# Streaming most of a kernel's modulation weights beside its first mixer instead of ahead of it

## What is computed

```python
def modulation(cond, w_ada, b_ada):
    m = jax.nn.silu(cond) @ w_ada + b_ada
    return jnp.split(m[:, None, :], 6, axis=-1)

for l in range(DEPTH):
    sh1, sc1, g1, sh2, sc2, g2 = modulation(cond, P['w_ada'][l], P['b_ada'][l])
    h = rms_norm(x, P['norm_mix'][l]) * (1 + sc1) + sh1
    out, new = even_mixer(...)          # layer 1: odd_mixer
    x = x + g1 * out
    h = rms_norm(x, P['norm_ffn'][l]) * (1 + sc2) + sh2
    x = x + g2 * peer(h, P, l)
```

## Time and profile before

| | us |
|---|---|
| median of 3 runs (lowest, highest) | 4934.05 (4928.89, 4938.43) |
| the profiled execution's own time | 4933.69 |
| its span, first to last instruction | 4931.8 |
| setup, to the first instruction of the norm | 232.0 |
| preparation | 53.4 |
| scan | 64.05 |

### The profile page before, as it was taken

One profiled execution on the slowest core, in us unless ns is written; L12 is line 12 of the kernel. 1 busy time (PEld: TensorE's weight loads), 2 busy tenths in 40 slices (PEclk: granted clock), 3 DMA queues, 4 the chain that ended last, 5 costly groups with the idle time before them and its releaser, 6 DMA issues. The chain is left out here.

```text
span 4931.8 us, 41363 instructions
## 1 busy us (share of the span) xinstructions
PE 3925.3 (80%) x11732; PEld 1816.5 (37%) x11732; DVE 3104.1 (63%) x8304; ACT 1053.6 (21%) x2804; POOL 2675.2 (54%) x2872
## 2 busy tenths in 40 slices
PE   6596698887877877877788988687878879778777
PEld 2354463332322322322256666433323223223222
DVE  0123757777777777676426556487777776776774
ACT  1202231111111111111235545111111111111111
POOL 1110006777777777777532322057777777777775
PEclk8996799999999999999999999799999999999999
DMA  9910129999999999999911011189999999999998
GB/s 391 370 56 10 41 106 354 397 399 405 386 409 405 387 407 400 392 405 409 333 50 48 24 47 36 78 312 401 398 409 396 402 403 395 409 407 392 409 409 347
DMA packets 456205, 1508.39 MB, mean 306 GB/s; under 512 B 50838, under 2 KB 99894, under 8 KB 455228
## 3 DMA queue, kind: packets, MB, share of 16 engines
q0 software_dynamic: 371104, 1347.37, 69.3%
q1 hardware_dynamic: 80284, 141.82, 8.0%
q10 hardware_dynamic: 4608, 16.78, 0.8%
HBM read 1484.84 MB, written 20.94 MB: 305 GB/s over the span
## 5 line engine op out<-in xcount | busy, mean ns | idle before, releaser
L627 PE MATMUL psall<-work 128*128 128x512 f32 x5120 | 2440.4, 607 | 655.8 <-DMA work<-in_p_v,idx 595.1
L435 DVE CUSTOM_DVE_ANT_0 work<-work,psall 128x1024 f32<-128x1024 f32 x1280 | 1518.6, 1219 | 850.4 <-DMA work<-in_p_u,idx 850.2
L348 POOL DMA_INDIRECT work<-in_p_u,idx x1280 | 1214.6, 949 | 926.0 <-DVE idx L413 455.0
L627 PEld LDWEIGHTS psall<-work 128*128 128x128 f32 x5120 | 889.7, 189 | 2201.5 <-issue 1102.9
L356 POOL DMA_INDIRECT work<-in_p_v,idx x1280 | 1218.9, 952 | 496.5 <-issue 317.3
L536 ACT ACTIVATE work<-ident,work 128x128 f32<-128x128 f32 x1280 | 487.4, 399 | 1932.5 <-PE psall L627 1899.8
L1407 PE MATMUL psall<-work 128*128 128x512 f32 x640 | 283.5, 596 | 9.0 <-ACT work L1499 5.2
L574 PE MATMUL psall<-work 128*128 128x512 f32 x640 | 278.2, 592 | 0.0
L1380 POOL TENSOR_SCALAR work<-work 128x256 f32<-128x256 f32 x40 | 33.8, 844 | 379.9 <-ACT work L1491 379.9
L1602 DVE TENSOR_TENSOR work<-psall,work 128x128 f32<-128x128 f32 x560 | 116.6, 285 | 100.3 <-ACT work L1518 100.3
L574 PEld LDWEIGHTS psall<-work 128*128 128x128 f32 x640 | 121.6, 190 | 153.1 <-issue 153.1
(11 more groups left out here) (274 smaller groups left out, 3706.1 us busy)
## 6 DMA issues: line engine op xcount, KB each, us to landing
work<-in_w_ada SPq DMA_DIRECT2D x64, 768.0 KB, 12.5
work<-in_p_u,idx POOLq DMA_INDIRECT x1280, 8.1
work<-in_p_v,idx POOLq DMA_INDIRECT x1280, 8.2
work<-in_o_w_in SPq DMA_DIRECT2D x40, 512.0 KB, 7.0
work<-in_p_w_qT SPq DMA_DIRECT2D x32, 512.0 KB, 14.1
wqk_rows<-work ACTq DMA_DIRECT2D x32, 512.0 KB, 7.4
work<-wqk_rows SPq DMA_DIRECT2D x2, 6144.0 KB, 20.3
work<-mod_rows SPq DMA_DIRECT2D x16, 512.0 KB, 5.9
```

Of the source, the lines that this page charges most:

```text
L348: nc.gpsimd.indirect_dma_start(m.ur[:, b, :], None, u_flat, bass.IndirectOffsetOnAxis(ap=e, axis=0)).then_inc(s.ud[b].h, 16)
L435: nc.vector.tensor_tensor_reduce(m.ur[:, b, :], m.ur[:, b, :], m.h2p[:, :], 1.0, 0.0, ALU.mult, ALU.add, m.d16[:, j:j + 1]).then_inc(s.ufr ...
L627: q = nc.tensor.matmul(o[:, k * 512:(k + 1) * 512], m.dgb[:, j % DIAGS, :], m.vr[:, b, k * 512:(k + 1) * 512], start=(i == 0 and j == 0), ...
```

## The change

Setup now computes only the first two groups, that is the first shift and scale of layer 0 (16 of the 64 loads); all 32 folds stand behind them. The other 48 loads' worth is cut anew into 12 "later" groups of eight pieces of 128 x 768 (384 KB), through a ring of four buffers. Groups 0 to 4 are worked off in the preparation, 5 to 11 in the scan. In both blocks SP issues the loads, TensorE makes three products of 2 x 256 per piece between its own work, all into one PSUM bank (7), ScalarE copies a finished group out (`later_keep`), and POOL, not VectorE, loads bias and norm rows, adds and multiplies, and stores to the same table (`later_rows`). A group's first product waits for the copy of the group before it (`s.ce`).

```diff
-GROUPS = 4 * DEPTH
+GROUPS = 2
+LATER = 12
+PIECE = 768
...
 def setup_order():
...
+    return [("w", n) for n in range(8 * GROUPS)] + [("f", f) for f in range(UNITS)]
...
+def is_scale(chunk):
+    return chunk // 4 in (1, 4)
+
+def later_load(m, sp, n):
+    l, chunk = later_group(n // 8)
+    if n >= WRING:
+        sp.wait_ge(s.wk.h, 8 * GROUPS + n - WRING + 1)
+    sp.dma_start(m.lwa[:, n % WRING, :], m.w_ada[l][n % 8 * P:(n % 8 + 1) * P, chunk * 256:chunk * 256 + PIECE]).then_inc(s.wq[n % WRING].h, 16)
+
+def later_product(nc, m, pe, n):
+    g, k = n // 8, n % 8
+    pe.wait_ge(s.wq[n % WRING].h, 16 * (8 * GROUPS // WRING + n // WRING + 1))
+    if k == 0 and g >= 1:
+        pe.wait_ge(s.ce.h, 1 + g)
+    for j in range(3):
+        q = nc.tensor.matmul(m.ps[7][32 * j:32 * j + 2, 0:256], m.condT[:, k, :], m.lwa[:, n % WRING, j * 256:(j + 1) * 256], start=(k == 0), stop=(k == KC - 1))
+    q.then_inc(s.wk.h, 1)
+
+def later_keep(nc, m, act, g):
+    act.wait_ge(s.wk.h, 8 * GROUPS + 8 * (g + 1))
+    if g >= 2:
+        act.wait_ge(s.modst.h, 16 * 3 * (GROUPS + g - 1))
+    for j in range(3):
+        q = nc.scalar.activation(m.lrow[32 * j:32 * j + 2, g % 2, :], m.ps[7][32 * j:32 * j + 2, 0:256], ACT.Copy)
+    q.then_inc(s.ce.h, 1)
+
+def later_rows(nc, m, pool, groups):
...
+    for g in groups:
+        bias(g)
+        l, chunk = later_group(g)
+        pool.wait_ge(s.const.h, m.n_const)
+        pool.wait_ge(s.ce.h, g + 2)
+        for j in range(3):
+            v = m.lrow[32 * j:32 * j + 2, g % 2, :]
+            nc.gpsimd.tensor_tensor(v, v, m.lbrow[32 * j:32 * j + 2, g % 2, :], ALU.add).then_inc(s.hr.h, 1)
+            s.hr.base += 1
+            if is_scale(chunk + j):
+                pool.wait_ge(s.hr.h, s.hr.base)
+                nc.gpsimd.tensor_scalar(v, v, 1.0, None, ALU.add).then_inc(s.hr.h, 1)
+                pool.wait_ge(s.hr.h, s.hr.base + 1)
+                nc.gpsimd.tensor_tensor(v, v, m.lnrow[32 * j:32 * j + 2, g % 2, :], ALU.mult).then_inc(s.hr.h, 1)
+                s.hr.base += 2
+        pool.wait_ge(s.hr.h, s.hr.base)
+        for j in range(3):
...
+            pool.dma_start(m.mod[first:first + 7:6, (c % 4) * 256:(c % 4) * 256 + 256], m.lrow[32 * j:32 * j + 2, g % 2, :]).then_inc(s.modst.h, 16)
+    pool.wait_ge(s.modst.h, 16 * 3 * (GROUPS + groups[-1] + 1))
+
+IN_PREPARE, IN_SCAN = range(0, 5), range(5, LATER)
...
 def even_prepare(nc, m, out):
...
+            for n in range(WRING):
+                later_load(m, sp, n)
...
             sp.wait_ge(s.nrm.h, 1)
...
+            for n in range(WRING, 8 * len(IN_PREPARE)):
+                later_load(m, sp, n)
...
                 nc.scalar.activation(m.kTd[:, :, t * P:(t + 1) * P], ...).then_inc(s.qte.h, 1)
+                if t >= 1:
+                    later_keep(nc, m, act, t - 1)
...
             nc.scalar.activation(m.z[:, :, :], m.z[:, :, :], ACT.Silu)
+            later_keep(nc, m, act, IN_PREPARE[-1])
...
+            later_rows(nc, m, pool, IN_PREPARE)
...
                 q.then_inc(s.qt.h, 1)
+                if t < TILES - 1:
+                    for n in range(8 * t, 8 * t + 8):
+                        later_product(nc, m, pe, n)
...
+            for n in range(8 * (TILES - 1), 8 * TILES):
+                later_product(nc, m, pe, n)
...
 def ssd_scan(nc, m, out):
...
+            first = 8 * IN_SCAN[0]
+            for n in range(first, first + 2 * WRING):
+                later_load(m, sp, n)
             sp.wait_ge(s.st.h, 2)
...
+            for n in range(first + 2 * WRING, 8 * LATER):
+                later_load(m, sp, n)
...
+            later_rows(nc, m, pool, IN_SCAN)
...
                 nc.tensor.matmul(m.ps[2 + b][:, :], m.bmt[:, t, :], m.xw[:, b, :], start=True, stop=True).then_inc(s.up.h, 1)
+                for i in range(4 * n, 4 * n + 4):
+                    later_product(nc, m, pe, 8 * IN_SCAN[0] + i)
+            for i in range(8 * IN_SCAN[0] + 4 * len(steps), 8 * LATER):
+                later_product(nc, m, pe, i)
...
+            for g in IN_SCAN[:5]:
+                later_keep(nc, m, act, g)
             for t in range(TILES):
...
+                if t in (1, 3):
+                    later_keep(nc, m, act, IN_SCAN[5 + t // 2])
```

More of the change, by code:

```diff
@@ L140, in _ @@
                 for r in range(2):
-                    for l in range(DEPTH):
-                        pool.dma_start(m.brow[32 * j + r:32 * j + r + 1, 4 * l:4 * l + 4, :],
-                                       m.b_ada[l:l + 1, :].rearrange("o (c j n) -> j o c n", j=3, n=512)[j]).then_inc(s.const.h, 16)
+                    pool.dma_start(m.brow[32 * j + r:32 * j + r + 1, :, :],
+                                   m.b_ada[0:1, :].rearrange("o (c j n) -> j o c n", j=3, n=512)[j][:, 0:GROUPS, :]).then_inc(s.const.h, 16)
+            for c in range(GROUPS):
+                p0 = 64 if c % 2 == 0 else 0
+                pool.dma_start(m.nrow[p0:p0 + 2, c, :], m.norm_mix[0:1, c * 512:c * 512 + 512].to_broadcast([2, 512])).then_inc(s.const.h, 16)
             for l in range(DEPTH):
[L145 to L148, removed]
                 pool.dma_start(m.keysT[:, l, :], m.p_keysT[l]).then_inc(s.keys.h, 16)
@@ L225, in _, with later_group @@
             ch.close()
+def later_group(g):
+    return (0, 12 + 3 * g) if g < 4 else (1, 3 * (g - 4))
+def is_scale(chunk):
+    return chunk // 4 in (1, 4)
+def later_load(m, sp, n):
+    s = m.sems
+    l, chunk = later_group(n // 8)
[3 more added lines that the diff above has]
+def later_product(nc, m, pe, n):
+    s = m.sems
+    g, k = n // 8, n % 8
[5 more added lines that the diff above has]
+    q.then_inc(s.wk.h, 1)
@@ new lines, in later_keep, with bias @@
+def later_keep(nc, m, act, g):
+    s = m.sems
+    act.wait_ge(s.wk.h, 8 * GROUPS + 8 * (g + 1))
[5 more added lines that the diff above has]
+def later_rows(nc, m, pool, groups):
+    s = m.sems
+    def bias(g):
+        l, chunk = later_group(g)
+        for j in range(3):
+            c = chunk + j
+            pool.dma_start(m.lbrow[32 * j:32 * j + 2, g % 2, :], m.b_ada[l:l + 1, c * 256:c * 256 + 256].to_broadcast([2, 256])).then_inc(s.const.h, 16)
+            m.n_const += 16
+            if is_scale(c):
+                row = (m.norm_mix, m.norm_ffn)[c // 12][l:l + 1, (c % 4) * 256:(c % 4) * 256 + 256]
+                pool.dma_start(m.lnrow[32 * j:32 * j + 2, g % 2, :], row.to_broadcast([2, 256])).then_inc(s.const.h, 16)
+                m.n_const += 16
+    for g in groups:
+        bias(g)
+        l, chunk = later_group(g)
+        pool.wait_ge(s.const.h, m.n_const)
[11 more added lines that the diff above has]
+        pool.wait_ge(s.hr.h, s.hr.base)
+        for j in range(3):
+            c = chunk + j
+            first = 12 * l + (1, 0, 2, 4, 3, 5)[c // 4]
+            pool.dma_start(m.mod[first:first + 7:6, (c % 4) * 256:(c % 4) * 256 + 256], m.lrow[32 * j:32 * j + 2, g % 2, :]).then_inc(s.modst.h, 16)
+    pool.wait_ge(s.modst.h, 16 * 3 * (GROUPS + groups[-1] + 1))
@@ L718, in even_memory @@
     m.pjunk = m.segs[0][:, 0, 0:4, :].rearrange("p h t -> p (h t)")
-    q = Arena(15360)
+    q = Arena(xp)
     m.pr = q.take(3, 512)
@@ L894, in _ @@
         def _(pool):
-            nc.gpsimd.memset(m.cmz[64:128, 0, :], 0.0)
-            nc.gpsimd.memset(m.cmz[0:64, 1, :], 0.0)
+            nc.gpsimd.memset(m.cmz[64:128, 0, :], 0.0).then_inc(m.sems.hr.h, 1)
+            nc.gpsimd.memset(m.cmz[0:64, 1, :], 0.0).then_inc(m.sems.hr.h, 1)
+            m.sems.hr.base += 2
+            pool.wait_ge(m.sems.hr.h, m.sems.hr.base)
+            later_rows(nc, m, pool, IN_PREPARE)
         @block.vector
@@ L1069, in _ @@
                     sp.dma_start(out["new_state_ssd"][0, 0, d, 4 * g:4 * g + 4].rearrange("h n p -> n h p"), m.stc[g * 64:(g + 1) * 64, d, :, :]).then_inc(s.so.h, 16)
+            for n in range(first + 2 * WRING, 8 * LATER):
+                later_load(m, sp, n)
             sp.wait_ge(s.so.h, 64)
+        @block.gpsimd
+        def _(pool):
+            later_rows(nc, m, pool, IN_SCAN)
         @block.tensor
@@ L1791, in build @@
         m.ce = r.take(16)
-        m.condT = r.take(KC, 2)
+        m.condT = sb("condT", [P, KC, 2])
+        r = Arena(15360)
+        m.lwa, m.lrow, m.lbrow, m.lnrow = r.take(WRING, PIECE), r.take(2, 256), r.take(2, 256), r.take(2, 256)
         m.ones = sb("ones", [P, P])
@@ L1823, in build @@
         odd_memory(nc, m, Arena, sb)
-        m.n_const = 16 * (len(m.const_loads) + 6 * DEPTH + 4 * DEPTH)
+        m.n_const = 16 * (len(m.const_loads) + 6 + GROUPS)
         setup_phase(nc, m)
```

## The result

The changed kernel takes 4953.78 us (median of 8 runs, 4951.28 to 4963.15) against 4935.24 (median of 8) for the kernel before in the same runs: slower by 0.4%, ratio 1.0041, 95% interval 1.0031 to 1.0052. The forecast was 4939, a change too small to tell from none. The time lies in the range of 4910 to 4972, but outside the 4924 to 4944 that the forecast gave as its own. The profiled execution took 4956.5 us, its span is 4954.7.

What follows compares the result with a forecast made beforehand. DMA bytes were taken to bound setup, and serial folds after the change. Setup -65.7, preparation +39.6 and scan +31.0 sum to +4.9 us: 4938.6 us, own range 4924 to 4944, wide range 4910 to 4972.

Steps and rivals of the forecast that it cites:

- one fold in ten at half clock: Setup: folds take 3.3 us at full clock, 4.9 at half; this mix gives 3.44 each, 110 us in all.
- fold-loop rival: Setup: folds lose the clock or meet their stores; 4952 us, or 4985 at half clock throughout; chance 0.11.
- The queue is a quarter idle: Setup: reason to take ScalarE's wait for the store of two folds ago as free, below a landing of 5.4 us.
- the rounds: Preparation: each tile is one serial round of loads, products, transposes, evacuation and keep, taken as 12 us.
- GpSimd's lag: Ends of preparation and scan: the next stage starts 5.7 us after POOL's last store was issued, as at setup's end.
- Step 9's update ends at 590: Scan: time of this update on the old clock, with its group kept at 593.5 us.
- 4.8: Scan, steps 3 to 9: us per step with four pieces each, rounds of 5.3 and 4.3 in turn; 4.43 before.
- the last 16 pieces end near 608: Scan's end: these pieces and VectorE's and ScalarE's tail finish near 608 us on the old clock, before POOL.
- group 9 starts when its rows have landed: Scan's end: POOL starts group 9 at 595.3 us; its chain through group 11 ends the stage at 628.4, +31 us.
- POOL becomes the bound: Rival, preparation and scan: a scale group takes 15.5 us against 9.8 per step pair; +46 and +45, 4960 us; chance 0.22.
- +7.7: Scan: us by which step 3's update ends later, near 561.5, behind state outputs, piece landings and products.
- The code load: Rival, preparation: code loading before POOL's first +1 of group 1, about 6 or 7 us, gives 4943 or 4944; chance 0.06.

Runs made afterwards that it cites:

- fold_pairs: The change with the folds alternating between two pairs of PSUM banks: 4952.11 us, ratio 1.0030 to the kernel before.
- deep_ring: The change with a ring of eight, three PSUM banks, merged early rows, ScalarE's state outputs and early copies, early scan pieces and products: 4897.85 us, 0.9925 to the kernel before.
- rows_early: The change with all twelve groups' bias and norm rows loaded once, at the preparation's start: 4945.10 us, ratio 1.0022 to the kernel before.
- experiment 6: The change with 60 more small, unused loads on GpSimd's queue at the preparation's start: 4957.63 us, ratio 1.0048 to the kernel before.

## Why the prediction was right, and where not

**Setup**, -65.7 forecast, -71.5 measured. The mechanism is as said: folds one behind another through one PSUM pair, no store in the way (fold_pairs shows that the store would be next). The term that was off is "one fold in ten at half clock": granted was 0.99 from 60 to 160 us, each fold took 3.29 instead of 3.44, and the first started at 51.4 instead of 53. The fold-loop rival falls. "The queue is a quarter idle" holds for the bytes, not for the engines' share of 0.84.

**Preparation**, +39.6 forecast, +42.1 measured. The first copy came 36.9 us into the stage (37.1 forecast), the rounds took 13.7, 12.4 and 13.4 (12), the fourth copy ended at 76.3 (73.1). GpSimd's lag was 4.4 instead of 5.7: it goes by the number of DMAs, 34 here and 51 in setup before, from which I took it. As forecast, GpSimd waited here for ScalarE, but for one wait of 2.7 us for rows.

**Scan**, +31.0 forecast, +42.6 measured. This is the step that failed, in three terms. "Step 9's update ends at 590", 56.7 us into the stage: it ended at 62.6, since steps 3 to 9 came 5.6 us apart instead of the "4.8" that I worked out from four pieces per step. TensorE waited there for landings, and neither two banks (5.4) nor early rows (5.5) nor both (5.8) nor the state outputs elsewhere (5.5) brought the steps clearly closer; deep_ring, with a ring of eight and its other edits, has 4.6. So landings set the steps; that the ring of four held them back is likely, but no run changes it alone. The same pace held behind the steps: "the last 16 pieces end near 608", 74.7 us into the stage, and the last copy ended at 88.4. And "group 9 starts when its rows have landed" put GpSimd one wait behind the copies; it had fallen behind them from its second group on, and touched the last group 8.4 us after its copy. A scale group took 13.8 to 15.6 us where I had 13.1, a group without scale 10.3 to 10.5 for 8.6 while loads ran. The wait for rows after the last issue was 3.2 to 4.6 us instead of 3.3, and the arithmetic of group 9 took 7.1 instead of 5.8 beside VectorE's tail. The rival "POOL becomes the bound" gave its point as a landing of about 4 us; here, on average 4.1, it decided, in the scan alone. rows_early, with that wait gone, takes the 95.1 us that I forecast, but that is luck: there the last copy, 87.0 us into the stage, sets the end, not the chain of GpSimd that I added up.

Step 3's update came 8.8 us later than before ("+7.7"), but that the state outputs make most of it is not shown: with them on ScalarE's queue it was still 6.2 later.

The three terms sum to +13.2 instead of +4.9; some 4 us outside them, which I had put at nothing, make most of what is left to the medians' +18.5. There is luck in the total: setup's 5.8 us in the change's favour hide half of the scan's 11.6. The time lies in the wide range because that was drawn to hold the GpSimd-bound rival, and it is nearer to that rival's 4960 than to the forecast's 4939, though the preparation got there without GpSimd as its bound.

**The code load.** GpSimd's configuration stands at 393.9, right behind an add and ahead of its first TENSOR_SCALAR:

```profile
L287 POOLq MODIFY_POOL_CONFIG  x2: 1/1/1, 393.9 to 393.9; - x2
```

```profile
392.44 1.51 POOL L283 TENSOR_TENSOR work<-work 2x256 f32<-2x256 f32 x2 [6.60 <-ACT work L257]
394.05 0.87 POOL L287 TENSOR_SCALAR work<-work 2x256 f32<-2x256 f32 x1
```

0.1 us lies between them, and the operation takes 0.87 where later ones take 0.84. The rule of the Trainium skill (GPSIMD Engine Reference, Instruction dispatch) of about 6 us for a first call does not show here; that rival is out. Whether any code was loaded at that instruction no row shows.

## What to carry to other kernels

A load moved into idle DMA time is cheap only if nothing on its new way is serial: streaming through one PSUM bank, a ring of four and rows that GpSimd asked for just before it needed them cost 85 us here, and 26 once it was given room. Taking one such wait away shows the next, so look for the chain behind it before counting the gain, and price a helper engine by its whole cycle, issues and waits, against the pace of the engine that feeds it. And when the DMA stops being the bound, ask what the loop left behind is bound by: the folds had 27 us in them that the bytes had hidden.

## What the runs showed that I had not expected

The end of a block in which GpSimd issues DMAs comes later by about 0.08 us for each of them, however early they were issued (4.4 us for 34, 9.3 for 94, experiment 6); the wait for the last stores is only 1.2 us of it. What GpSimd does in that time no row shows.

VectorE's operations with both inputs in SBUF grow longer while GpSimd computes. An addition of 128x512 in the scan's tail, grouped over 576 to 592 us, in the changed kernel (first) and before (columns: busy us, mean ns, idle before):

```profile
L1216 DVE TENSOR_TENSOR work<-work 128x512 f32<-128x512 f32 x3 | 3.4, 1125 | 0.3
```

```profile
L1114 DVE TENSOR_TENSOR work<-work 128x512 f32<-128x512 f32 x4 | 2.8, 692 | 0.4
```

At 575.16 us, while loads stream as well but GpSimd waits, the same line takes 0.69. GpSimd's own TENSOR_SCALAR takes up to 1.17 us there instead of 0.84. The Trainium skill (GPSIMD Engine Reference, Specifications) names this contention for VectorE's instructions with two SBUF inputs, and the trace agrees. My forecast had left it out.
